# Last attention of a one-core float32 transformer kernel: eighths of the output product moved behind the loop, scores two at a time in the freed banks, transposes on two bank pairs

## The reference

```python
    imp = jnp.where(blk > cur, -1.0, jnp.where(forced, FORCE_SCORE, imp))
    _, sel_idx = lax.top_k(imp, top)
    q_rot = rope(q, pos)
...
        p_sel = masked_softmax(jnp.einsum('bkgqd,bkqmd->bkgqm', qc, ks) * scale,
                               kpos <= qpos[:, None])
        o_sel = jnp.einsum('bkgqm,bkqmd->bkgqd', p_sel, vs)
...
        p_win = masked_softmax(jnp.einsum('bkgqd,bknd->bkgqn', qc, kw) * scale, win_mask)
        o_win = jnp.einsum('bkgqn,bknd->bkgqd', p_win, vw)
...
    o = gates[0] * o_cmp + gates[1] * o_sel + gates[2] * o_win
    o = o.transpose(0, 3, 1, 2, 4).reshape(Bsz, S, NSA_HEADS * Dh).astype(h.dtype)
    return o @ w_o
```

## Time and profile before

| | |
|---|---|
| median of the runs | 1328.27 us |
| the profiled execution, its own time | 1327.78 us |
| its span (first to last instruction) | 1326.1 us |
| PE busy, share of the span | 1312.4 us, 99% |
| DVE | 969.2 us, 73% |
| ACT | 751.3 us, 57% |
| POOL | 123.7 us, 9% |
| share of PE in the chain that ended last | 86% |

### The profile page before, as it was taken

The page is one execution under the profiler, slowest core; times in us unless marked ns, Lnnn a source line. Parts: engine busy times, 40 slices in busy tenths (PEclk is TensorE's granted clock), DMA queues, the critical chain, the costliest instruction groups (busy, mean ns, idle before and its releaser), DMA issues.

```text
span 1326.1 us, 20799 instructions
## 1 busy us (share of the span) xinstructions
PE 1312.4 (99%) x7581; PEld 1127.9 (85%) x7581; DVE 969.2 (73%) x1503; ACT 751.3 (57%) x1210; POOL 123.7 (9%) x123
## 2 busy tenths in 40 slices
PE   9999999999999999999999999999999999999998
PEld 8987888889988888888889878888889877888886
DVE  5767765657746657665668768998878985899885
ACT  6645554546345545454566347666657756776663
POOL 0101000002500100000001310000003234000000
PEclk9999999999999999999999999999999999999999
DMA  7545656565653474656545345566546422456661
GB/s 258 190 131 194 233 176 211 170 212 165 194 191 127 157 225 152 222 170 214 171 156 203 128 161 172 186 203 192 190 153 208 146 78 65 158 173 211 195 191 58
DMA packets 64023, 231.62 MB, mean 175 GB/s; under 512 B 7104, under 2 KB 7360, under 8 KB 63936
## 3 DMA queue, kind: packets, MB, share of 16 engines
q1 hardware_dynamic: 62208, 224.42, 52.0%
q10 hardware_dynamic: 1728, 6.00, 1.3%
HBM read 229.34 MB, written 1.05 MB: 174 GB/s over the span
## 4 chain that ended last, share of the span: by engine, by line
PE 86%; DVE 9%; ACT 3%; issue 1%; DMA 0%; POOLq 0%; POOL 0%; SPq 0%; DVEq 0%
PE ps L580 18%; PE ps L633 17%; PE ps L582 17%; PE ps L581 17%; PE ps L641 9%; DVE w_lo L1835 3%; PE ps L1004 1%; DVE x_both L1855 1%; ACT w_hi L1305 1%; PE ps L1196 1%; PE ps L552 1%; PE ps L1165 1%; DVE arena L2002 1%; DVE arena L2007 1%; PE ps L1178 1%
## 5 line engine op out<-in xcount | busy, mean ns | idle before, releaser
L1835 DVE TENSOR_TENSOR w_lo<-ring,w_hi 128x1024 fp32r<-128x1024 f32 x423 | 517.4, 1255 | 131.4 <-ACT w_hi L1305 131.1
L1305 ACT ACTIVATE w_hi<-ring 128x1024 fp32r<-128x1024 f32 x423 | 432.1, 1054 | 182.3 <-PE ps L582 151.3
L633 PE MATMUL ps<-x_both,w_hi 128*128 128x512 f32 x1216 | 293.6, 392 | 1.7 <-DVE arena L1989 1.2
L633 PEld LDWEIGHTS ps<-x_both,w_hi 128*128 128x128 f32 x1216 | 223.4, 188 | 48.2 <-DVE arena L1989 2.0
L580 PE MATMUL ps<-w_hi,y_hi 128*128 128x512 f32 x560 | 220.3, 393 | 0.4 <-DVE y_lo L1887 0.4
L581 PE MATMUL ps<-w_lo,y_hi 128*128 128x512 f32 x560 | 218.3, 390 | 0.0
L582 PE MATMUL ps<-w_hi,y_lo 128*128 128x512 f32 x560 | 218.1, 389 | 0.0
L641 PEld LDWEIGHTS ps<-x_both,w_lo 128*128 128x128 f32 x1216 | 157.5, 191 | 7.0
L641 PE MATMUL ps<-x_both,w_lo 128*128 128x256 f32 x1216 | 159.6, 282 | 0.0
L582 PEld LDWEIGHTS ps<-w_hi,y_lo 128*128 128x128 f32 x560 | 105.1, 188 | 22.3
L580 PEld LDWEIGHTS ps<-w_hi,y_hi 128*128 128x128 f32 x560 | 105.3, 188 | 22.0 <-issue 0.8
(11 more groups left out here) (242 smaller groups left out, 1521.9 us busy)
## 6 DMA issues: line engine op xcount, KB each, us to landing
ring<-ws SPq DMA_DIRECT2D x424, 512.0 KB, 4.8
tab<-tables ACTq DMA_DIRECT2D x3, 572.0 KB, 5.9
rowg<-rows ACTq DMA_DIRECT2D x3, 512.0 KB, 6.5
h<-x SPq DMA_DIRECT2D x4, 256.0 KB, 6.1
out<-arena SPq DMA_DIRECT2D x4, 256.0 KB, 2.2
arena<-decay ACTq DMA_DIRECT2D x1, 768.0 KB, 10.6
sm<-small ACTq DMA_DIRECT2D x1, 642.0 KB, 4.8
arena<-narrow ACTq DMA_DIRECT2D x1, 512.0 KB, 6.8
```

The costliest lines, as they stand in the source:

```text
L633: mm(ps[:, b + j, :], w_hi[:, s, c:c + P], x_both[:, k, :, :], start=k == 0, stop=False, skip_group_check=True)
L1305: A(w_hi[:, q // 2 % RING, c:c + HALF], ring[:, q % RAW, :], ACT.Copy).then_inc(hi_ready, 1)
L1835: V.tensor_tensor(w_lo[:, g % RING, v], ring[:, q % RAW, :], w_hi[:, g % RING, v].bitcast(F32), ALU.subtract).then_inc(lo_ready, 1)
```

## The change

PE no longer issues fills in the loop's turns 2 to 5: three stand in turn 6 ahead of its `ns_pv`, two behind it, three in turn 7, and twelve behind the loop. Banks 0 to 3 are free until then, and the scores of one branch go to 0 and 1, of the other to 2 and 3, both `ns_qk` of a turn together. Transposes of even steps stay in banks 6 and 7, those of odd steps from 5 on go to 4 and 5, where the outputs of pairs 3 to 7 go as well. The orders of ACT and DVE are changed to fit, and the splits of pieces `+ 17` and `+ 18` move: `+ 17` to turn 6, `+ 18` behind the loop.

```diff
@@ -197,7 +197,18 @@
         ns_xhf, ns_xlf = ns_xf[:, 0:KT * T], ns_xf[:, KT * T:2 * KT * T]
         ns_xh, ns_xl = (x[:, 0:1920].rearrange("p (i l n) -> p i l n", i=2, n=60) for x in (ns_xhf, ns_xlf))
         ns_cmp_at = ps[:, 4:6, 384:512]
-        ns_o = ps[:, 6:8, 384:512]
+        def ns_score_bank(it):
+            return 4 if it < 6 else 2 * (it % 2)
+
+        def ns_turn_bank(it):
+            return 4 if it >= 5 and it % 2 else 6
+
+        def ns_out_bank(pr):
+            return 4 if pr >= 3 else 6
+
+        def ns_o(pr):
+            return ps[:, ns_out_bank(pr):ns_out_bank(pr) + 2, 384:512]
+
         ns_bank = (3, 0, 4, 5)
 
         loaded, rest_loaded, narrow_in = sem("small_loaded"), sem("small_rest_loaded"), sem("narrow_loaded")
@@ -1152,30 +1163,40 @@
                 if it < 2:
                     pe.wait_ge(nsa_kd_other, it + 1)
                     pe.wait_ge(nsa_sin, 2)
-                if it >= 5:
-                    pe.wait_ge(nsa_cmp_scores_copied, 1 if it < 6 else 2)
-                if it >= 6:
-                    pe.wait_ge(nsa_cmp_pT_copied, 1 if it < 10 else 2)
+                if it == 5:
+                    pe.wait_ge(nsa_cmp_scores_copied, 1)
+                if it == 6:
+                    pe.wait_ge(nsa_sin, 6)
                 pe.wait_ge(nsa_roped, pr // 2 + 1)
-                if it:
-                    pe.wait_ge(nsa_max, it)
+                if it and it not in (6, 7):
+                    pe.wait_ge(nsa_max, it if it < 6 else it - 1)
                 for t in range(TT):
                     for i in range(2):
                         v = slice(64 * i, 64 * i + 64)
-                        r = mm(ps[:, 4 + i, P * t:P * (2 * t + 1)], ns_qr[v, pr, t * P:(t + 1) * P],
+                        r = mm(ps[:, ns_score_bank(it) + i, P * t:P * (2 * t + 1)], ns_qr[v, pr, t * P:(t + 1) * P],
                                ns_kd[v, br, pr // 2, 0:P * (t + 1)], start=t == 0, stop=True, skip_group_check=True)
                 r.then_inc(nsa_scores, 1)
 
             def ns_t(it):
                 pe.wait_ge(nsa_p, it + 1)
                 if it:
-                    pe.wait_ge(nsa_pT_copied, it)
-                    pe.wait_ge(nsa_pT_copied2, it)
-                if it >= 4:
-                    pe.wait_ge(nsa_oT_lo, max(it // 2, 2))
+                    pe.wait_ge(nsa_pT_copied, it - 1 if it > 4 else it)
+                    pe.wait_ge(nsa_pT_copied2, it - 1 if it > 4 else it)
+                if it == 4:
+                    pe.wait_ge(nsa_oT_lo, 2)
+                if it == 5:
+                    pe.wait_ge(nsa_max, 6)
+                    pe.wait_ge(nsa_cmp_scores_copied, 2)
+                    pe.wait_ge(nsa_cmp_pT_copied, 1)
+                if it == 6:
+                    pe.wait_ge(nsa_oT_lo, 3)
+                if it == 7:
+                    pe.wait_ge(nsa_cmp_pT_copied, 2)
+                if it > 7 and it % 2:
+                    pe.wait_ge(nsa_oT_lo, it // 2)
                 for i in range(2):
                     for j in range(3):
-                        r = nc.tensor.transpose(ps[:, 6 + i, j * P:(j + 1) * P],
+                        r = nc.tensor.transpose(ps[:, ns_turn_bank(it) + i, j * P:(j + 1) * P],
                                                 ns_s[it][:, i, j * P:(j + 1) * P], ident)
                 r.then_inc(nsa_pT, 1)
 
...
@@ -1208,7 +1229,7 @@
                     filled[0] += 1
                     i, k, t, j = (n // 8, n // 4 % 2, n // 2 % 2, n % 4) if n < 16 else (2, n // 2 % 2, 0, n % 2)
                     if n == 0:
-                        pe.wait_ge(nsa_sin, 6)
+                        pe.wait_ge(nsa_max, 16)
                     if (k, n) in ((0, 8 * i), (1, 8 * i + 4), (1, 18)):
                         pe.wait_ge(nsa_oT_lo, 2 * i + k + 1)
                         split(G_NSA + 14 + i, k)
@@ -1257,25 +1278,21 @@
             ns_cmp_qk(1)
             ns_pv(1)
             ns_qk(6)
-            ns_fill(1)
             ns_qk(7)
-            ns_fill(1)
             for pr in range(2, 8):
                 ns_t(2 * pr)
-                if pr == 2:
-                    ns_fill(1)
+                ns_t(2 * pr + 1)
                 if pr < 6:
                     ns_qk(2 * pr + 4)
-                ns_fill(1 if pr < 6 else 2)
-                ns_t(2 * pr + 1)
-                if pr < 6:
                     ns_qk(2 * pr + 5)
                 else:
-                    ns_fill(2)
+                    ns_fill(3)
                 ns_pv(pr)
                 if pr == 2:
                     ns_cmp_t(1)
-                ns_fill((0, 1, 1, 1, 2, 0)[pr - 2])
+                if pr == 6:
+                    ns_fill(2)
+            ns_fill(12)
             pe.wait_ge(nsa_oT_lo, 7)
             close([(G_NSA + 16, (4, 5)), (G_NSA + 17, (6, 7))], 8, {(1, 1): (nsa_oT_lo, 8)}, src=(x_hi, x_lo), begun=1)
             hidden(8, ffn_h[1], ffn_s[0], ffn_s[1], None, FFN_TILES)
...
@@ -1774,20 +1791,18 @@
             ns_hi(1)
             ns_exp(6)
             for pr in range(2, 8):
-                it = 2 * pr
-                ns_copy(it)
                 if pr < 7:
-                    ns_exp(it + 3)
-                ns_copy(it + 1)
+                    ns_exp(2 * pr + 3)
+                ns_copy(2 * pr)
+                ns_copy(2 * pr + 1)
                 if pr < 6:
-                    ns_exp(it + 4)
+                    ns_exp(2 * pr + 4)
                 ns_hi(pr)
                 if pr == 2:
                     ns_cmp_copy(1)
-                if pr in (2, 4):
-                    act.wait_ge(done, G_NSA + 13 + pr // 2)
-                if pr < 6:
-                    hi_half(2 * (G_NSA + 17) + pr - 2)
+                if pr == 6:
+                    hi(G_NSA + 17)
+            refill(G_NSA + 14)
             refill(G_NSA + 15)
             norm(8, G_NSA + 16, G_NSA + 17)
             spread(8, scale)
...
@@ -2537,17 +2552,23 @@
             ns_scores(7)
             lo_half(2 * (G_NSA + 16) + 1)
             for pr in range(2, 8):
-                for it in (2 * pr, 2 * pr + 1):
-                    ns_copy(it)
-                    if it % 2 and 2 < pr < 7:
-                        lo_half(2 * (G_NSA + 17) + pr - 3)
-                    if it + 4 < 16:
-                        ns_scores(it + 4)
-                    if it + 2 < 16:
-                        ns_coef(it + 2)
+                if pr < 7:
+                    ns_coef(2 * pr + 2)
+                ns_copy(2 * pr)
+                ns_copy(2 * pr + 1)
+                if pr < 7:
+                    ns_coef(2 * pr + 3)
+                if pr < 6:
+                    ns_scores(2 * pr + 4)
+                    ns_scores(2 * pr + 5)
+                if pr == 6:
+                    lo_half(2 * (G_NSA + 17))
                 ns_lo(pr)
                 if pr == 2:
                     ns_roped(3)
+                if pr == 6:
+                    lo_half(2 * (G_NSA + 17) + 1)
+            refill(G_NSA + 14)
             refill(G_NSA + 15)
             residual(8, G_NSA + 17, 8)
             norm(8, G_NSA + 16, G_NSA + 17)
```

More of the change, by code:

```diff
@@ L1142, in ns_cmp_t @@
                 pe.wait_ge(nsa_cmp_p, c + 1)
-                pe.wait_ge(nsa_max, 6 + 4 * c)
+                pe.wait_ge(nsa_max, 6)
                 for t in range(TT):
@@ L1189, in ns_pv @@
                 for t in range(TT):
-                    mm(ns_o[:, t, :], ns_vbd[:, pr // 4, 2 * (pr % 4):2 * (pr % 4) + 2, :], ns_cp[:, 2 * (pr // 4) + t, :],
+                    mm(ns_o(pr)[:, t, :], ns_vbd[:, pr // 4, 2 * (pr % 4):2 * (pr % 4) + 2, :], ns_cp[:, 2 * (pr // 4) + t, :],
                        start=True, stop=False, skip_group_check=True)
@@ L1195, in ns_pv @@
                         for i in range(2):
-                            r = mm(ps[64 * i:64 * i + 64, 6 + t, 384:512], v[:, s, :],
+                            r = mm(ps[64 * i:64 * i + 64, ns_out_bank(pr) + t, 384:512], v[:, s, :],
                                    ns_p[(2 * pr + br) % 4][:, i, n * P:(n + 1) * P], start=False,
@@ L1714, in ns_copy @@
                     act.wait_ge(nsa_o, it // 2 - 1)
-                A(ns_p[it % 4][:, 0, :], ps[:, 6, 0:384], ACT.Copy).then_inc(nsa_pT_copied, 1)
+                A(ns_p[it % 4][:, 0, :], ps[:, ns_turn_bank(it), 0:384], ACT.Copy).then_inc(nsa_pT_copied, 1)
             def ns_hi(pr):
                 act.wait_ge(nsa_o, pr + 1)
-                A(x_hi[:, pr, :].rearrange("p (t n) -> p t n", n=P), ns_o, ACT.Copy).then_inc(nsa_oT_hi, 1)
+                A(x_hi[:, pr, :].rearrange("p (t n) -> p t n", n=P), ns_o(pr), ACT.Copy).then_inc(nsa_oT_hi, 1)
             def ns_kd_other(br):
@@ L2432, in ns_scores @@
                         v = slice(P * t, P * t + P * (t + 1))
-                        r = V.tensor_tensor_reduce(ns_s[it][:, i, v], ps[:, 4 + i, v],
+                        r = V.tensor_tensor_reduce(ns_s[it][:, i, v], ps[:, ns_score_bank(it) + i, v],
```

(4 more changed lines are left out.)

## The result

The changed kernel takes 1330.97 us (median of 12 runs, 1330.73 to 1332.81), the kernel before 1328.15 on the same chip (12 runs, 1327.59 to 1328.67). The ratio is 1.0024, 95% interval 1.0016 to 1.0033: slower by 2.8 us, just beyond the 0.2% (2.7 us) that the prediction took for telling from no change, which lies inside the interval. Forecast were 1332.5 and a range of 1330.0 to 1335.0.

A forecast was written before the change was run, and what follows sets the result against it. The prediction took the loop to be limited by what PE has to issue. Its terms, 3.7 - 0.25 + 0.8 = 4.25 us, took the profiled 1327.78 to 1332.0, and with 0.49 for the median to 1332.5 us, range 1330.0 to 1335.0.

The forecast's parts named there:

- The cover in turn 2: Scores to transposes of step 6: DVE decides, ending 0.2 us earlier with four fills fewer; PE waits some 4.5 us.
- The circle in turns 3 to 5: Odd transposes wait for the previous turn's output through DVE and ACT: 5.80 us a turn, above PE's 5.16.
- Turn 6, the split behind half a piece: DVE splits half of piece +17 ahead of ns_lo: output to transposes 3.23 us instead of 1.10; PE waits 1.1.
- The close: Twelve fills give DVE time, so the first wait of PE's residual transposes goes: 0.25 us, between 0 and 0.5.
- DVE while POOL works: Odd steps' coefficients fall into POOL's scaling of even steps; 0.8 us taken, between bounds of 0 and 1.55.
- The row with 0.17 of 0.32: Line 2355, earlier trace: one instruction during POOL's work took 0.86 us, three others 0.69; 0.17 of a possible 0.32.
- the 1.55 us: Upper bound of POOL's term, full port wait: 0.5 + 0.45 + 0.3 + 0.3; the sum would be 0.75 us longer.
- the clock lost for turns 3 to 5: Rival: clock falls as PE waits, PE's 5.16 us doubles to 10.3 in each turn; 1346 us; 4 in 100.
- That PE stays busy: Rival: scores issued two at a time keep PE from waiting for the split; about -2.8, 1325.5 us; 6 in 100.
- That it evens out: Rival: waits come to 4 us instead of 7.5; 1328.5 us (1327 to 1330); 9 in 100.

The follow-up runs named there:

- clock kept: Changed kernel plus fifteen idle PE products (identity with itself) at PE's three waits of turn 2; 1331.02 us, ratio 1.0021.
- POOL-later: Changed kernel, but POOL starts scaling even steps 6 to 14 only once the odd step's coefficients are there too; 1331.93 us, ratio 1.0028.
- the split first: Changed kernel with DVE's ns_lo of pair 6 ahead of both halves of piece +17 instead of between them; 1330.59 us, ratio 1.0018.
- one edit: Kernel before with DVE's second half of piece +19 behind the first two parts of the new residual instead of ahead; 1327.91 us against 1328.14.
- four more edits: Changed kernel with ns_lo of pair 6 first, POOL's scaling later, idle products in turn 2, half of piece +16 moved to turn 6; 1329.43 us.

## Why the prediction was right

The forecast was a sum over stretches of PE's time. Here it stands, with POOL's 0.8 shared out as it was derived (0.25 in the first stretch, 0.52 in the second), against the changed kernel with the clock kept, and against its own profile (us):

| stretch | forecast | clock kept | own profile |
|---|---|---|---|
| scores of step 6 to transposes of step 6 | 11.89 | 11.79 | 11.79 |
| to transposes of step 13 | 18.52 | 17.82 | 19.17 |
| to the norm's transposes | 25.54 | 25.09 | 25.10 |
| sum | 55.95 | 54.70 | 56.06 |

Before it was 51.80 (1077.46 to 1129.26). So with the clock kept this part costs +2.90, as the medians do (+2.8). (The clock-kept kernel's profiled execution, 1331.38, lies 3.6 above; 0.7 of that stands ahead of the scores of step 6, which start at 1078.19.) The clock cost 1.35 more in the changed kernel's own profile. That this execution lies 4.3 above the profiled one of before, and the forecast was 4.25, is an accident: the clock, which the forecast had at nothing, filled in for terms that it had too long. Where the forecast's stretches carry 4.15, the rest is rounding. Against the median the forecast of 1332.5 is 1.5 too high. Of these, 0.10, 0.70 and 0.45 are the three stretches of the table, and the rest is rounding and the base, 1328.27 where 12 runs gave 1328.15.

*What bounds the kernel before.* Misread, without harm to the sum. The prediction took the loop for limited by what PE has to issue, with no other engine near. But without any fill a turn still took 7.16 us, and DVE and ACT were busy 6.18 and 6.21 of 7.30 us. A nearly full PE was full of filler that stood in waits.

*The cover in turn 2.* Right. Three waits of 4.42 us in all, forecast 4.5, at the places named. That the part is as long as before (11.79 against 11.88) doesn't mean that it ends by the same chain. ACT's last read of the exponentials of step 8 and its split of pair 2, first before, then in the changed kernel:

```profile
1087.44 0.19 ACT L1707 ACTIVATION_READ_ACCUMULATOR arena<-arena 128x1 f32 x1
1088.36 0.38 ACT L1719 ACTIVATE x_both<-ps 128x256 fp32r<-128x256 f32 x1 [0.73 <-PE ps L1196]
```

```profile
1088.28 0.19 ACT L1724 ACTIVATION_READ_ACCUMULATOR arena<-arena 128x1 f32 x1
1088.37 0.36 ACT L1736 ACTIVATE x_both<-ps 128x256 fp32r<-128x256 f32 x1
```

Before, the exponentials were through and the split waited 0.73 us for PE's output. Now PE's output has long been there, and the split waits for the exponentials, which the new order of DVE starts later. In the run with the fills moved alone, transposes of step 5 stand 6.63 us behind the scores of step 6 instead of 7.07; so without its fills the old order would have been some 0.4 us shorter here (an estimate, as the clock fell behind it), and the new order took that back.

*The circle in turns 3 to 5.* Right in kind and nearly in size: 5.72 against 5.80. The difference is in masked scores and exponentials, 2.99 against 1.11 + 1.86 + 0.1. Doubling PE's transposes didn't move it and adding to DVE did. A second branch, PE's scores, ties with DVE's copy and coefficients: 0.77 + 0.98 in the POOL-later kernel (1095.58, 1096.35, 1097.33) against 0.88 + 0.47 + 0.40. So shortening only one of them gives nothing.

*Turn 6, the split behind half a piece.* Right: 0.88 against 1.1; with the split first it is gone. Twelve fills took 8.30 (1121.22 to 1129.52) against 8.39.

*The close.* Mis-sized: close to norm is 4.08 (1129.52 to 1133.60) against 4.49 before, a gain of 0.41 where I took 0.25 of a possible 0.5. The kernel before gets 0.27 of it from one edit.

*DVE while POOL works.* The term is mis-sized, 0.8 us for some 0.45, by a reading of the earlier trace rows that failed. DVE and POOL do not meet only at semaphores: DVE's product waits for the end of POOL's instruction, in full. POOL scales a step in two instructions, 0.61 and 1.00 long; in both cases the product met the second. It ended at 1083.83 + 1.61 = 1085.44 in turn 2 and at 1098.89 in turn 4, and the products of 1084.80 and 1098.62 ended at 1085.45 and 1098.91. The overlap forecast was 0.5 in turn 2 and 0.3 in turn 4; it is 0.64 and 0.27. But in these two cases a quarter us of the overlap doesn't reach the path: start to next start was 0.58 and 0.21, against 0.19 free, that is 0.39 and 0.02 more. POOL-later agrees, with 0.42 in turn 2 and nothing in the others. The row with 0.17 of 0.32 can be read as the same effect and no half lock: counted from POOL's end, that row, the products and the half piece of 2.13 us (POOL's end at 1088.41) are all some 0.15 shorter than alone. That an instruction gets as much done ahead of the lock is my reading, and no run takes it apart. A lock for a whole instruction is what the Trainium skill states for this pair ("SBUF — State Buffer", SBUF: two separate sides). These rows agree with it, but not with the 1.55 us that I had put beside it as the price.

*The clock.* The rival was the clock lost for turns 3 to 5, 1346, with 4 in 100. It did not happen so, but a smaller form did that I hadn't priced: a fall for some 3.5 us, 1.35 us long in the profiled execution. My ground against it, that 1.1 us without work in 11.9 kept the clock before, said little on 4.4 us in 11.8. What such a fall costs depends on where it lies: it was 0.50 and 0.27 us in the profiles with doubled transposes and with the split first, where it slowed work that a wait follows: the bracket ahead of the transposes of step 6 is 0.67 and 0.47 us there instead of 1.77. The median of the changed kernel hardly moves by it: 1330.97 against 1331.02 with the clock kept. What decides in which execution the clock falls is open.

*The other rivals.* That PE stays busy (1325.5) fell with the waits. That it evens out (1328.5) was to be decided at 4.0 us of waits; in the profile there are 4.42 + 0.23 + 0.46 + 0.46 + 0.88 = 6.45. The nearest forms that did come close to even, 1329.43, needed four more edits.

## What to carry to other kernels

Filler inside the waits of an engine that works in order is free there and costs its full length elsewhere: before moving it, find the chain on the other engines that ended the wait, and see whether it too gets shorter by what is taken out. An engine that is busy 98% of a stretch need not be its limit: take the filler out and look. Doubled buffers shortened the turn here only to the circle over DVE and ACT, 5.72 us, so they gave back 4 of the 6.9 us that the move cost. And small edits that each remove a wait have to be run together, since one may put its work under another's.
